# New durations in a planner's account of engine times, and another order of mixer 2's projections

## What is computed

```python
def first_block(h):                         # feed-forward, mixer 1, feed-forward
    h = h + 0.5 * rmsnorm(swiglu(rmsnorm(h)))                    # inner width 2816
    z, xbc, dt, q, k, v, gates = split(rmsnorm(h) @ w_in)
    y_ssd = ssd_branch(z, xbc, dt)          # state space, 32 heads in 4 groups, chunks of 128
    y_att = diff_attn_branch(q, k, v)       # 8 heads of differential attention
    h = h + rmsnorm((gates[0] * y_ssd + gates[1] * y_att) @ w_out)
    return h + 0.5 * rmsnorm(swiglu(rmsnorm(h)))

def second_block(h):                        # mixer 2, feed-forward
    g_qkv, g_z, a, b, q, k, v, iq, ik, iw, gate_a, gate_b = split(rmsnorm(h) @ w_in_2)
    o_gdn = gated_delta_rule(l2norm(silu(conv(g_qkv))), a, b)    # 8 heads, chunks of 64
    o_gdn = rmsnorm(o_gdn) * silu(g_z)
    score = sum_h(iw[h] * relu(iq[h] @ layernorm(ik).T))         # 8 index heads, causal
    keep = top_k(score, 128)
    o_dsa = softmax(q @ k.T where keep) @ v                      # 8 heads, 2 key-value heads
    h = h + (sigmoid(gate_a) * o_gdn + sigmoid(gate_b) * o_dsa) @ w_out_2
    return rmsnorm(h + (silu(f_gate) * f_val) @ w_down)          # f: conv(rmsnorm(h) @ w_up)
```

## Time and profile before

| | us |
|---|---|
| median of 3 runs | 2481.38 |
| lowest and highest | 2481.28, 2483.11 |
| the profiled execution, its own time | 2481.96 |
| its span in the profile | 2480.2 |
| granted clock of the profiled execution, mean | 0.998 of full |

### The profile page before, as it was taken

The page is one execution under the profiler, slowest core; times in us unless marked ns, Lnnn a source line. Parts: engine busy times, 40 slices in busy tenths (PEclk is TensorE's granted clock), DMA queues, the critical chain, the costliest instruction groups (busy, mean ns, idle before and its releaser), DMA issues.

```text
span 2480.2 us, 41294 instructions
## 1 busy us (share of the span) xinstructions
PE 2449.9 (99%) x17114; PEld 2036.4 (82%) x17114; DVE 1614.0 (65%) x2597; ACT 1220.1 (49%) x2057; POOL 75.5 (3%) x114
## 2 busy tenths in 40 slices
PE   9999999999999999999999999999999999999998
PEld 7999888887877777887999888877777778888887
DVE  6888338866765645257888438778778556677733
ACT  6555335765556556346555436653633454444421
POOL 0111000000000000000111000000000000000000
PEclk9999999999999999999999999999999999999999
DMA  5776332222222222322677333212211112332232
GB/s 168 179 182 163 102 99 88 85 77 77 76 70 77 69 68 69 102 94 80 163 186 170 100 93 99 86 44 62 69 46 59 45 43 85 99 97 94 89 102 73
DMA packets 80394, 237.51 MB, mean 96 GB/s; under 512 B 8912, under 2 KB 10960, under 8 KB 80208
## 3 DMA queue, kind: packets, MB, share of 16 engines
q1 hardware_dynamic: 68688, 213.03, 27.6%
q0 software_dynamic: 10080, 18.35, 4.9%
q10 hardware_dynamic: 1440, 3.49, 0.4%
HBM read 232.75 MB, written 2.10 MB: 95 GB/s over the span
## 4 chain that ended last, share of the span: by engine, by line
PE 90%; DVE 5%; ACT 3%; issue 1%; DMA 1%; SPq 0%; ACTq 0%; DVEq 0%
PE bank L2390 21%; PE bank L2392 20%; PE bank L2391 20%; PE bank L2404 4%; PE bank L2405 4%; PE bank L2406 4%; PE bank L2659 1%; DVE hl L3213 1%; PE bank L2584 1%; PE bank L2565 1%; ACT hl L2825 1%; PE bank L2592 1%; PE bank L2776 1%; PE bank L2578 1%; PE bank L2419 0%
## 5 line engine op out<-in xcount | busy, mean ns | idle before, releaser
L2390 PE MATMUL bank<-uR,hl 128*128 128x512 f32 x1676 | 677.4, 404 | 5.4 <-DVE uR L3224 2.5
L3213 DVE TENSOR_TENSOR hl<-raw,hl 128x1024 fp32r<-128x1024 f32 (+1 forms) x324 | 384.8, 1190 | 432.8 <-ACT hl L2825 431.7
L2392 PE MATMUL bank<-uR,hl 128*128 128x512 f32 x1676 | 655.8, 391 | 0.0
L2391 PE MATMUL bank<-uR,hl 128*128 128x512 f32 x1676 | 655.6, 391 | 0.0
L2825 ACT CAST hl<-raw 128x1024 fp32r<-128x1024 f32 (+1 forms) x324 | 328.8, 1019 | 209.3 <-PE bank L2392 200.6
L2390 PEld LDWEIGHTS bank<-uR,hl 128*128 128x128 f32 x1676 | 315.6, 188 | 87.9 <-issue 17.6
L2392 PEld LDWEIGHTS bank<-uR,hl 128*128 128x128 f32 x1676 | 315.5, 188 | 67.5
L2391 PEld LDWEIGHTS bank<-uR,hl 128*128 128x128 f32 x1676 | 315.9, 188 | 63.7 <-issue 3.3
L3207 DVE TENSOR_TENSOR hl<-raw,hl 128x1024 fp32r<-128x1024 f32 (+1 forms) x142 | 150.7, 1075 | 30.7 <-ACT hl L2821 27.0
L2404 PE MATMUL bank<-sum,hl 128*128 128x256 f32 x560 | 159.3, 284 | 1.9 <-DVE fA L3391 1.8
L2405 PE MATMUL bank<-sum,hl 128*128 128x256 f32 x560 | 158.8, 283 | 0.0
(11 more groups left out here) (608 smaller groups left out, 4368.1 us busy)
## 6 DMA issues: line engine op xcount, KB each, us to landing
raw<-in_win SPq DMA_DIRECT2D x146, 512.0 KB, 3.5
raw<-in_w SPq DMA_DIRECT2D x44, 512.0 KB, 3.5
raw<-in_w1u SPq DMA_DIRECT2D x54, 256.0 KB, 3.2
raw<-in_w2u SPq DMA_DIRECT2D x51, 256.0 KB, 3.3
raw<-in_w1g SPq DMA_DIRECT2D x22, 512.0 KB, 4.7
raw<-in_w2g SPq DMA_DIRECT2D x22, 512.0 KB, 4.6
raw<-in_w1d SPq DMA_DIRECT2D x16, 512.0 KB, 3.6
raw<-in_wssd SPq DMA_DIRECT2D x16, 512.0 KB, 3.5
```

Of the source, the lines that this page charges most:

```text
L2390: e.matmul(s.bank[:, :], h[:, 0, w], hi, start=s.first and q == 0, stop=False)
L2391: e.matmul(s.bank[:, :], h[:, 0, w], lo, start=False, stop=False)
L2392: i = e.matmul(s.bank[:, :], h[:, 1, w], hi, start=False, stop=s.last and q == n - 1)
L3213: e.tensor_tensor(h[:, 1, w], x[:, w], h[:, 0, w].bitcast(F), ALU.subtract).then_inc(*sig("dve_split.lo", s, i))
```

## The change

Three constants change: AHEAD2 from 6 to 8, BEHIND from 4 to 2, and TURN (0.1 for each change) gives way to INTO = 0.09 and BACK = 0.22. These are charged only between whole-array and partial products, by a list of the kinds of steps that use part of the array. In the table of durations some 30 entries get new numbers, most of them smaller; the diff shows six. ORDER2 places the sparse queries and the gates in another order. And `project_head` of mixer 1 now waits for a free page before it takes one. The computation is the same.

```diff
-AHEAD, AHEAD2 = 6.0, 6.0
+AHEAD, AHEAD2 = 6.0, 8.0
-BEHIND = 4.0
+BEHIND = 2.0
-TURN = 0.1
+INTO, BACK = 0.09, 0.22
+TILED = ("scan_s", "scan_v", "gdn_level", "gdn_fold", "gdn_seed_turn", "gdn_join", "gdn_corner", "gdn_w", "gdn_u",
+         "gdn_att", "gdn_decay", "narrow_turn", "att_front", "sp_front", "ix_score", "ssd_y", "decay_turn")
-ORDER2 = "n p0 x p1 z0 p2 z1 p3 z2 d0 d1 k z3 d2 d3 d4 d5 d6 d7 m0 m1 m2 m3 m4 m5 m6 m7"
+ORDER2 = "n p0 x p1 z0 p2 z1 p3 d0 z2 d1 k d2 d3 z3 d4 d5 d6 d7 m0 m1 m2 m3 m4 m5 m6 m7"
...
-        return [("PE", 0.2 * w, "pe_idx.score", 1), ("ACT", 0.4 + 0.22 * w), ("DVE", 0.2 + 0.32 * w, "dve_idx.score", 1)]
+        return [("PE", 0.27 * w, "pe_idx.score", 1), ("ACT", 0.4 + 0.22 * w), ("DVE", 0.2 + 0.32 * w, "dve_idx.score", 1)]
...
-        return [("PE", 0.14 * w), ("DVE", 0.2 + 0.135 * w), ("ACT Exp", 0.4 + 0.11 * w, "act_spa.P")]
+        return [("PE", 0.2 * w), ("DVE", 0.15 + 0.135 * w), ("ACT Exp", 0.25 + 0.09 * w, "act_spa.P")]
...
-    "ssd_state": [("PE", 3.2, "pe_ssd.state", 3), ("ACT", 0.6, "act_ssd.state"), ("DVE", 1.4, "dve_ssd.state", 2),
+    "ssd_state": [("PE", 2.18, "pe_ssd.state", 3), ("ACT", 0.6, "act_ssd.state"), ("DVE", 1.4, "dve_ssd.state", 2),
...
-    "gdn_level": [("PE", 0.6, "pe_gdn.Y"), ("ACT", 0.4, "act_gdn.Y"), ("DVE", 0.3, "dve_gdn.mask")],
-    "gdn_fold": [("PE", 1.2, "pe_gdn.fold"), ("DVE", 0.42, "dve_gdn.T"), ("DVE", 0.42, "dve_gdn.U")],
+    "gdn_level": [("PE", 0.68, "pe_gdn.Y"), ("ACT", 0.4, "act_gdn.Y"), ("DVE", 0.3, "dve_gdn.mask")],
+    "gdn_fold": [("PE", 1.24, "pe_gdn.fold"), ("DVE", 0.42, "dve_gdn.T"), ("DVE", 0.42, "dve_gdn.U")],
...
-    "gdn_out": [("PE", 1.6), ("DVE", 1.9, "dve_gdn.out")],
+    "gdn_out": [("PE", 0.87), ("DVE", 1.6, "dve_gdn.out")],
...
-            if engine == "PE" and clock["tiled"] != (s.kind != "mm"):
-                clock["tiled"] = s.kind != "mm"
-                t += TURN
+            if engine == "PE" and clock["tiled"] != (s.kind in TILED):
+                clock["tiled"] = s.kind in TILED
+                t += INTO if clock["tiled"] else BACK
...
         for name, j in (("q", 40 + h), ("k", 48 + h), ("v", 56 + h)):
             b = yield from ugemm(WIN[j])
+            yield from room(1)
             Hd[name] = evict("qkv_ev", b, scale=0.125 / slope_of(h) if name == "q" else None)
```

More of the change, by code:

```diff
@@ L144, in costs @@
     if k == "split":
-        return [("ACT", 1.0, "act_split.hi"), ("DVE", 1.2, "dve_split.lo")]
+        return [("ACT", 0.95, "act_split.hi"), ("DVE", 1.14, "dve_split.lo")]
     if k == "fold":
@@ L153, in costs @@
     if k == "conv":
-        return [("ACT", 0.7), ("DVE", 0.78 * (s["taps"] - 1), "dve_conv.tap", s["taps"] - 1)]
+        return [("ACT", 0.6), ("DVE", 0.745 * (s["taps"] - 1), "dve_conv.tap", s["taps"] - 1)]
     if k == "keep":
@@ L170, in costs @@
     if k == "pv_turn":
-        return [("PE", 0.1 + 0.11 * w, "pe_att.turn"), ("ACT", 0.2 + 0.09 * w, "act_att.A")]
+        return [("PE", 0.11 * w, "pe_att.turn"), ("ACT", 0.14 + 0.09 * w, "act_att.A")]
     if k == "pv_mul":
-        return [("PE", 0.25 * w, "pe_att.pv"), ("ACT", 0.28, "act_att.o")]
+        return [("PE", 0.23 * w, "pe_att.pv"), ("ACT", 0.28, "act_att.o")]
     if k == "ix_score":
-        return [("PE", 0.2 * w, "pe_idx.score", 1), ("ACT", 0.4 + 0.22 * w), ("DVE", 0.2 + 0.32 * w, "dve_idx.score", 1)]
+        return [("PE", 0.27 * w, "pe_idx.score", 1), ("ACT", 0.4 + 0.22 * w), ("DVE", 0.2 + 0.32 * w, "dve_idx.score", 1)]
     if k == "ix_top":
@@ L188 @@
     "product": [("PE", 1.44, "pe_gemm.mm")], "act_split": [("ACT", 0.62), ("DVE", 0.69, "dve_ffn.lo")],
-    "fast_x": [("ACT", 0.73, "act_fast.x")], "fast_scale": [("DVE", 0.69, "dve_fast.scale")], "fast_sum": [("DVE", 1.2, "dve_fast.sum")], "fast_hi": [("ACT", 1.0, "act_fast.sum_hi")],
+    "fast_x": [("ACT", 0.73, "act_fast.x")], "fast_scale": [("DVE", 0.69, "dve_fast.scale")], "fast_sum": [("DVE", 1.2, "dve_fast.sum")], "fast_hi": [("ACT", 0.95, "act_fast.sum_hi")],
     "fast_lo": [("DVE", 1.2, "dve_fast.sum_lo")],
@@ L216 @@
     "ssd_x": [("PE", 0.44, "pe_ssd.x"), ("DVE", 0.69, "dve_ssd.x")],
-    "ssd_cb": [("PE", 0.44), ("PE", 1.2, "pe_ssd.cb"), ("ACT", 2.4, "act_ssd.Y", 3), ("ACT", 0.6, "act_ssd.BN"),
+    "ssd_cb": [("PE", 0.44), ("PE", 0.82, "pe_ssd.cb"), ("ACT", 2.4, "act_ssd.Y", 3), ("ACT", 0.6, "act_ssd.BN"),
                ("DVE", 0.69, "dve_ssd.CB")],
@@ L220 @@
     "ssd_front": [("PE", 0.23), ("ACT Exp", 1.1, "act_ssd.E")],
-    "ssd_mask": [("DVE", 0.75, "dve_ssd.E")],
-    "ssd_state": [("PE", 3.2, "pe_ssd.state", 3), ("ACT", 0.6, "act_ssd.state"), ("DVE", 1.4, "dve_ssd.state", 2),
+    "ssd_mask": [("DVE", 0.65, "dve_ssd.E")],
+    "ssd_state": [("PE", 2.18, "pe_ssd.state", 3), ("ACT", 0.6, "act_ssd.state"), ("DVE", 1.4, "dve_ssd.state", 2),
                   ("DVE", 1.4, "dve_ssd.state", 3)],
-    "ssd_from": [("PE", 1.3, "pe_ssd.off"), ("ACT Exp", 0.65, "act_ssd.EA"), ("DVE", 0.56, "dve_ssd.EA"), ("DVE", 0.56, "dve_ssd.off")],
+    "ssd_from": [("PE", 0.92, "pe_ssd.off"), ("ACT Exp", 0.65, "act_ssd.EA"), ("DVE", 0.56, "dve_ssd.EA"), ("DVE", 0.56, "dve_ssd.off")],
     "ssd_y": [("PE", 1.03, "pe_ssd.y"), ("DVE", 0.69, "dve_ssd.y")],
@@ L229 @@
     "narrow_turn": [("PE", 4.1, "pe_gdn.iw"), ("ACT Exp", 2.2, "act_gdn.cols", 1), ("ACT", 0.6, "act_gdn.iw")],
-    "l2": [("DVE", 0.75, "dve_gdn.l2")],
+    "l2": [("DVE", 0.65, "dve_gdn.l2")],
     "gdn_decay": [("PE", 1.0), ("DVE", 0.69, "dve_gdn.seg"), ("DVE", 0.43), ("ACT Exp", 0.65, "act_gdn.gm")],
@@ L235 @@
     "gdn_seed": [("DVE", 1.6, "dve_gdn.U0"), ("DVE", 0.4, "dve_gdn.A", 0), ("DVE", 0.4, "dve_gdn.A", 1)],
-    "gdn_seed_turn": [("PE", 0.6), ("ACT", 0.4, "act_gdn.T")],
-    "gdn_level": [("PE", 0.6, "pe_gdn.Y"), ("ACT", 0.4, "act_gdn.Y"), ("DVE", 0.3, "dve_gdn.mask")],
-    "gdn_fold": [("PE", 1.2, "pe_gdn.fold"), ("DVE", 0.42, "dve_gdn.T"), ("DVE", 0.42, "dve_gdn.U")],
+    "gdn_seed_turn": [("PE", 0.68), ("ACT", 0.4, "act_gdn.T")],
+    "gdn_level": [("PE", 0.68, "pe_gdn.Y"), ("ACT", 0.4, "act_gdn.Y"), ("DVE", 0.3, "dve_gdn.mask")],
+    "gdn_fold": [("PE", 1.24, "pe_gdn.fold"), ("DVE", 0.42, "dve_gdn.T"), ("DVE", 0.42, "dve_gdn.U")],
     "gdn_corner": [("PE", 0.6), ("ACT", 0.8, "act_gdn.corner")],
@@ L243 @@
     "scan_v": [("PE", 0.4), ("DVE", 0.3, "dve_gdn.vn")],
-    "scan_s": [("PE", 1.1, "pe_gdn.o"), ("DVE", 0.35, "dve_gdn.state", 0), ("DVE", 0.35, "dve_gdn.state", 1),
-               ("DVE", 0.6, "dve_gdn.o")],
-    "gdn_norm": [("ACT", 1.25), ("DVE", 1.0, "dve_gdn.sum"), ("ACT Ln", 0.45), ("DVE", 1.4, "dve_gdn.on")],
-    "gdn_out": [("PE", 1.6), ("DVE", 1.9, "dve_gdn.out")],
+    "scan_s": [("PE", 1.1, "pe_gdn.o"), ("DVE", 0.28, "dve_gdn.state", 0), ("DVE", 0.28, "dve_gdn.state", 1),
+               ("DVE", 0.5, "dve_gdn.o")],
+    "gdn_norm": [("ACT", 1.25), ("DVE", 1.5, "dve_gdn.sum"), ("ACT Ln", 0.45), ("DVE", 1.4, "dve_gdn.on")],
+    "gdn_out": [("PE", 0.87), ("DVE", 1.6, "dve_gdn.out")],
     "ik_mean": [("PE", 0.9), ("DVE", 0.69, "dve_idx.mean")], "ik_norm": [("DVE", 0.75, "dve_idx.ik")],
```

## The result

The changed kernel takes 2501.03 us (median of 4 runs, 2497.39 to 2502.79) against 2481.33: a ratio of 1.0078, with a 95% interval of 1.0066 to 1.0090. It is slower by 19.7 us; I had forecast 9.2 more than the median before, with a range that ended at 2499. The direction was right, and the size that I gave was half of what it is. Three executions (3432 us in e11_mixer1_new, 6507 in e13_ahead55, 3430 among the 13 of before beside e1 to e4) took far longer than all others and are left out of the medians, except the last, which moves its median by 0.1 us.

What follows compares the result with a forecast made beforehand. PE was taken to bound the kernel, including its instruction fetch in the ladders. Terms -1.8 + 5 + 3.5 + 1.5 + 0.8 = +9.0 us on 2481.4 gave 2490.4, rounded to 2490.5, range 2481 to 2499.

Steps and rivals of the forecast that it cites:

- What bounds the kernel: Whole kernel: PE is busy 2449.9 of 2480.2 us, so time changes only by what happens on PE.
- Fewer switches: Mixer 2: twelve fewer rounds between whole-array and partial products on PE, -1.8 us (-2.5 to -0.9).
- The ladders: Mixer 2's head-pair ladders: denser small matmuls outrun instruction packets of 127 matmuls per 3.6 us, +5 us (+2 to +7.5).
- The clock: Behind the first ladder's stops: the half-clock stretch may come twice, +0.8 us (-1.7 to +3.4).
- The end of mixer 2: Last sparse-head steps: later mask and fewer projections between them make PE wait, +3.5 us (0 to +8).
- The rest: Rest of the order: grouped norms at mixer 2's start, +1.5 us (-2 to +4); mixer 1 0, plus or minus 1.
- A: Rival for both mixers: the account is simply better, engine waits and switches fall, 2476.5 us; chance 0.08.
- B: Rival: gains and losses cancel, for instance because fetch hides most of the new ladders, 2483 us; chance 0.16.
- C: The forecast itself, 2487 to 2494 us; chance 0.54.
- D: Rival at mixer 2's end: ACT's and DVE's queues hold every head, +8 there, 2496 to 2499 us; chance 0.22.
- E: Rival: only the order of mixer 2's projections matters and the account moves nothing; no chance of its own.

Runs made afterwards that it cites:

- e11_mixer1_new: Changed kernel with mixer 1 by the new account, mixer 2 by that of before, with AHEAD2, BEHIND and ORDER2 of before: 2486.22 us, ratio 1.0021.
- e13_ahead55: Kernel before with AHEAD2 = 5.5 in place of 6: 2506.60 us, ratio 1.0107.
- e1: Kernel before with 32 more 32x32 matmuls at the program's start, shifting the packet edges; order of steps unchanged: 2482.77 us, ratio 1.0007.
- e4: Changed kernel with mixer 1 planned by the account of before and mixer 2 by the new one: 2493.49 us.
- e9: Kernel before with levels and folds written as 16 matmuls of 64 columns for 32 of 32: 2468.99 us, ratio 0.9953.
- e10: Changed kernel with levels and folds written as 16 matmuls of 64 columns for 32 of 32: 2477.28 us, ratio 0.9986.
- e2: 512 small 32x32 products added in a row ahead of mixer 2's output projection: stops 128 matmuls and 3.48 us apart; no total time given.
- e8: Kernel before with BEHIND = 2 alone: 2494.57 us, +15.2.
- e7: Kernel before with AHEAD2 = 8 alone: 2490.04 us, +10.7.
- e5: Kernel before with the new ORDER2 alone: 2479.94 us, ratio 1.0001.
- e12_paced: Changed kernel with a planner rule spacing levels and folds 0.5 us behind a level and 1.2 behind a fold: 2500.66 us, +19.9.

## Why the prediction was off, point by point

**What bounds the kernel: right.** The time moved by PE's idle time and its clock, and whole-array products are still 0.23 us apart at full clock.

**Fewer switches, -1.8: it fits, but isn't shown.** What is left of mixer 2's difference without idle time and clock is -1.6; between e9 and e10 it is -1.3 (568.2 less 5.7 against 572.2 less 11.0). But in the kernels with 79 to 82 rounds in mixer 2 (84 before, 72 after) length without idle time and clock goes from 565.7 to 571.3, against 568.5 before, so something other than the switches moves it too.

**The ladders, +5: right in mechanism and nearly in size.** Stops went from 5.5 to 11.6 us, +6.1, and where they follow each other they stand 127 or 128 matmuls apart as forecast; e1, e2, the landings in the DMA records, e9 and e10 each show that it is the packets. Two things were wrong in it. The packet isn't 3.6 us long at all times: the second and fourth stop of the first ladder come 5.1 and 5.0 us behind the one before. And the 1.4 us wait at L2733 shows that the list of waits may name another engine for it. The Trainium skill (Runtime: NRT & Kernel Launch, Instruction fetch mechanics) calls fetching mostly hidden; in e2_dense it isn't hidden: 128 matmuls take 3.48 us, of which PE works 1.3 to 1.9.

**The clock, +0.8: the step that failed.** I had priced it by how often it would come, "it may come twice", with +3.4 as the upper bound. It came as 17.0 us at half clock in place of 3.4, a loss of 8.5 in place of 1.7: +6.8, twice the bound. The mechanism was named, and its link to the stops; but I took the one stretch of before as nearly independent of the stops' size, though it stood behind the longest of them. The ladders' stops of 1.5 to 2.5 us each had one here. The traces together show how strongly size matters. In the fifteen other than e2_dense PE idles for 1 us or more 107 times between 700 and 2100 us. All 16 waits of over 2 us have half clock in them or begin it within 2.5 us behind them; of the 91 shorter ones 18 do. With the ladders the term is 12.9 by the trace and 11.4 by e9 and e10, against 5.8 forecast.

**The end of mixer 2, +3.5: right in size and place.** 0.6 to 3.8 us, +3.2, before the turns and products that I had named. But I put it down to BEHIND; e8 bears that out (7.5 us), and e7 shows that AHEAD2 does the same or more (9.7 us, 5.8 of it in one wait). That the late mask is the reason was not tested.

**The rest, +1.5: right for mixer 2, wrong for mixer 1.** In mixer 2 the l2 norms' and the index key's waits (L2493, L2501) are there, +2.2 net, +0.3 at the boundary. Mixer 1 was taken as 0, plus or minus 1, since single steps move there; two of these moves put a split ahead of a softmax on DVE, and that is 2.5 us in the trace, 2.5 to 5.6 in five traces and 5.4 by the median of e11_mixer1_new, again with the clock. A move by a single step can't be priced at nothing. The second feed-forward adds 1.1 in this trace; it takes 356.5 to 357.6 in the others, 357.3 also in e2 and e8, whose order there is that of before, so most of this is scatter.

**Sum.** -1.6 + 6.1 + 6.8 + 3.2 + 2.2 + 0.3 + 2.5 + 1.1 = 20.6 for the profiled execution, which is 20.4 longer in its span.

**Rivals.** A and B fell, and C, the forecast, ended at 2494. D ("the end binds") had nearly the right time, 2496 to 2499, but by another price: its +8 at the end did not come. E is refuted by e5.

## What to carry to other kernels

A planner's numbers and the order that they give are one thing: numbers nearer to the trace are a new draw, and here all seven new accounts of mixer 2 were worse than the old. Judge the order, not the numbers. In a stretch of tiny matmuls count instructions as well as columns, and price every idle stop of over 1 us on PE with the clock that it can cost behind it, in all stages, above all one of over 2 us: here that was about as much as the new packet stops themselves.

## What the runs showed of the hardware

- An instruction packet of 128 small matmuls with their weight loads took 3.48 us in a long row of them (e2_dense), at full and at half clock. In the ladders of all traces, issue stops one packet apart are 3.3 to 5.4 us apart.
- PE goes on 1.19 to 1.60 us behind the landing of the packet (90 stops in fourteen traces). In e2_dense the next packet starts 1.0 to 1.4 us after that.
- In the changed kernel's first ladder two stops came 5.1 and 5.0 us behind the one before. There the packet started 2.6 us behind that stop, so the extra 1.5 us lie ahead of its transfer. A load of weights was under way in one of the two and none in the other; what held it back stays open.
- PE had enough in hand for 219 small matmuls behind whole-array work before its first stop (e2_dense).
- Half clock stood in or behind waits of 1.1 to 5.8 us, start and end of the program aside, for 3.4 or 6.8 us (once 10.2, and 23.9 in e2_dense). The same wait of 1.38 us had it in two of the five traces with the new mixer 1 (e11_mixer1_new and e12_paced) and not in the other three.
- Products of 32x32 tiles with 64 columns take less than two with 32: 1.03 (e9_wide_before) against 1.24 us for a fold.
